# Layer A's probabilities turned by VectorE and transfers instead of TensorE, with k in runs of 32 tokens

## What is computed

```python
qkv = (x @ a_w_qkv[layer]).reshape(B, S, 3, A_HEADS, A_HEAD_DIM)
q = partial_rotary(qkv[:, :, 0], positions).transpose(0, 2, 1, 3)
k = partial_rotary(qkv[:, :, 1], positions).transpose(0, 2, 1, 3)
v = qkv[:, :, 2].transpose(0, 2, 1, 3)
o = moba_attention(q, k, v).transpose(0, 2, 1, 3).reshape(B, S, D)
x = layer_norm(DEEPNORM_ALPHA * x + o @ a_w_o[layer], ln_g[layer, 0], ln_b[layer, 0])
...
s_own = jnp.einsum("bhqd,bhkd->bhqk", qc, k_own) * scale   # masked causally
p = softmax(s_own)
o = jnp.einsum("bhqk,bhkd->bhqd", p, v)
```

## Time and profile before

| | |
|---|---|
| median of 3 runs (lowest, highest) | 606.54 us (605.67, 606.56) |
| profiled execution: device time | 606.49 us |
| its span in the trace | 604.7 us |
| mean granted TensorE clock | 0.996 of full speed |
| first mixer, from the first scores to the last transposes of probabilities | 48.7 to 102.6 us |
| HBM read | 108.23 MB, 181 GB/s over the span |

### The profile page before, as it was taken

The page is one execution under the profiler, slowest core; times in us unless marked ns, Lnnn a source line. Parts: engine busy times, 40 slices in busy tenths (PEclk is TensorE's granted clock), DMA queues, the critical chain, the costliest instruction groups (busy, mean ns, idle before and its releaser), DMA issues.

```text
span 604.7 us, 8638 instructions
## 1 busy us (share of the span) xinstructions
PE 594.5 (98%) x3252; PEld 503.9 (83%) x3252; DVE 456.6 (76%) x817; ACT 328.3 (54%) x532; POOL 56.1 (9%) x83
## 2 busy tenths in 40 slices
PE   8999999999999999999999999999999999999995
PEld 6877777898888888889878888889888888888894
DVE  4877864877777887777688797778777777777756
ACT  5666776355544445455436587945555455554430
POOL 6200000400000000000520003132000000000002
PEclk9999999999999999999999999999999999999998
DMA  8898643253666676555537965442845556755501
GB/s 309 283 301 255 190 139 140 89 207 122 209 209 209 209 234 239 185 182 189 199 102 240 295 159 206 140 139 72 277 158 190 184 183 221 248 189 187 181 1 69
DMA packets 86709, 114.03 MB, mean 189 GB/s; under 512 B 19292, under 2 KB 64652, under 8 KB 86668
## 3 DMA queue, kind: packets, MB, share of 16 engines
q1 hardware_dynamic: 85228, 109.28, 54.7%
q0 software_dynamic: 1152, 4.19, 2.1%
q10 hardware_dynamic: 288, 0.00, 0.0%
HBM read 108.23 MB, written 1.05 MB: 181 GB/s over the span
## 4 chain that ended last, share of the span: by engine, by line
PE 91%; DVE 3%; DMA 2%; POOL 2%; issue 1%; ACT 1%; DVEq 0%; ACTq 0%
PE wide L1215 16%; PE wide L1217 16%; PE wide L1216 16%; PE score L1400 11%; PE score L1403 6%; PE turn L1400 5%; PE outb L1400 5%; PE outb L1403 3%; PE turn L1403 3%; DMA raw<-in_a_w_qkv 1%; PE turn L1302 1%; DVE w_lo L917 1%; PE outb L1320 1%; PE score L1217 1%; PE score L1216 1%
## 5 line engine op out<-in xcount | busy, mean ns | idle before, releaser
L917 DVE TENSOR_TENSOR w_lo<-raw,w_hi 128x2048 fp32r<-128x2048 f32 (+1 forms) x118 | 209.0, 1788 | 70.7 <-ACT w_hi L726 70.7
L726 ACT ACTIVATE w_hi<-raw 128x2048 fp32r<-128x2048 f32 (+1 forms) x126 | 182.2, 1483 | 32.3 <-PE wide L1217 23.2
L1215 PE MATMUL wide<-w_hi,xT 128*128 128x512 f32 (+1 forms) x256 | 96.2, 376 | 1.3 <-DVE w_lo L983 0.7
L1215 PE MATMUL wide<-w_hi,oT_hi 128*128 128x512 f32 x240 | 95.5, 398 | 0.2 <-DVE oT_lo L1162 0.2
L1216 PE MATMUL wide<-w_lo,oT_hi 128*128 128x512 f32 x240 | 93.7, 390 | 0.0
L1217 PE MATMUL wide<-w_hi,oT_lo 128*128 128x512 f32 x240 | 93.6, 390 | 0.0
L1217 PE MATMUL wide<-w_hi,xT 128*128 128x512 f32 (+1 forms) x256 | 93.1, 364 | 0.0
L1216 PE MATMUL wide<-w_lo,xT 128*128 128x512 f32 (+1 forms) x256 | 93.0, 363 | 0.0
L1400 PE MATMUL score<-xT,w_hi 128*128 128x512 f32 x288 | 71.8, 391 | 0.0
L848 ACT ACTIVATE qT<-kT,conv_cols 128x256 f32<-128x256 f32 x36 | 21.7, 602 | 87.7 <-DVE kT L1128 87.7
L1400 PEld LDWEIGHTS score<-xT,w_hi 128*128 128x128 f32 x288 | 52.8, 188 | 10.1
(11 more groups left out here) (176 smaller groups left out, 805.3 us busy)
## 6 DMA issues: line engine op xcount, KB each, us to landing
raw<-in_ffn_w_in SPq DMA_DIRECT2D x44, 1024.0 KB, 5.2
raw<-in_ffn_w_out SPq DMA_DIRECT2D x22, 1024.0 KB, 5.0
raw<-in_a_w_qkv SPq DMA_DIRECT2D x9, 1024.0 KB, 6.6
raw<-in_w_kv_shared SPq DMA_DIRECT2D x8, 1024.0 KB, 5.7
raw<-in_a_w_o SPq DMA_DIRECT2D x4, 1024.0 KB, 4.8
raw<-in_b_w_q SPq DMA_DIRECT2D x4, 1024.0 KB, 5.1
raw<-in_b_w_o SPq DMA_DIRECT2D x4, 1024.0 KB, 5.1
raw<-in_a_w_qkv SPq DMA_DIRECT2D x4, 512.0 KB, 7.8
```

The source lines that it names most:

```text
L726: ins = nc.scalar.activation(w_hi[c % RING][:, part], raw[c % RAW_RING][:, part], ACT.Copy)
L917: ins = nc.vector.tensor_tensor(w_lo[c % RING][:, part], raw[c % RAW_RING][:, part], w_hi[c % RING][:, part].bitcast(F32), ALU.subtract)
L1215: nc.tensor.matmul(dst, a_hi, b_hi, start=start, stop=False, skip_group_check=True)
```

## The change

The three transposes per map on TensorE and the copy on ScalarE leave the first mixer. In their place VectorE turns a map's 384 columns in 32x32 tiles with one instruction (`prob_turn`, L1103 of the changed kernel), writing so that the 32-query blocks of four maps (a **set**; `BATCH` is 4) lie together. Each 32x32 tile takes every fourth column of `probs`. Once four maps are turned, SyncE moves the set with four SBUF-to-SBUF transfers of 32 partitions each (`prob_move`, L559), 1.5 KB a partition. There are two buffers at each end (`STAGES` is 2): the sets leave from `norm_rows` (later the gain and shift of the norm) and `turned` (shared with q and k), and arrive in `probsT` and in a new buffer, `spare`, in which the small buffers of the second mixer have been put. Since a tile takes every fourth column, the key tokens come out in another order, and k (not q) is laid out in `kT` in runs of 32 tokens where tokens were interleaved. The moving operand of the scores is then four runs of 32 for each token tile.

In the planner, `prob_turn` and `prob_move` take the place of `probT` and `probT_out`, loads have become steps of their own on SyncE, and the tables of numbers are new, for both layers: the second mixer is computed by the same instructions as before, but they stand in another order.

```diff
+BATCH, STAGES = 4, 2
...
-    "move": ("SP", 5.0),
+    "move": ("SP", 3.1),
+    "load": ("SP", 0.4),
+    "prob_turn": ("DVE", 0.6),
+    "prob_move": ("SP", 3.1),
...
+        add(("load", c + RAW_RING), ("split_lo", c, 1))
...
-        add(("exp", m), ("mask", m), ("probT", m - 4 if A else m // 2 - 2))
+        add(("exp", m), ("mask", m), ("prob_turn", m - 4) if A else ("probT", m // 2 - 2))
...
+        if A:
+            add(("prob_turn", m), ("norm", m), ("prob_move", m // BATCH - STAGES))
+            if m // BATCH % 2 and BATCH == 4:
+                after[("prob_turn", m)].append(("move", max(n for n, (mat, _) in enumerate(COLUMNS) if mat < 2)))
+            if m % BATCH == BATCH - 1:
+                n = m // BATCH
+                add(("prob_move", n), ("prob_turn", m), *[("pv", PAIR_GROUP[h // 2]) for h in range(BATCH * n - 8, BATCH * n - 8 + BATCH) if h >= 0])
+        elif m % 2:
...
-            add(("pv", n), *[("probT_out", h) for h in PV_GROUPS[n]], ("drain", column(2, g), 1), ("out_lo", n - 1))
+            add(("pv", n), ("prob_move", PV_GROUPS[n][-1] // BATCH), ("drain", column(2, g), 1), ("out_lo", n - 1))
...
+        spare = sb("spare", [P, BATCH * 3 * P])
...
+        probsT_A = [probsT[:, :, :].rearrange("p s k -> p (s k)"), spare[:, :]]
...
+        prob_stage = [norm_rows[:, 0:BATCH * 3 * P], turned[:, :, :, :].rearrange("p n b q -> p (n b q)")[:, 0:BATCH * 3 * P]]
+        prob_stage = [stage.rearrange("p (b s k q) -> p b s k q", b=4, s=BATCH, k=3) for stage in prob_stage]
...
-                    sp.dma_start(headT[mat][:, 4 * g:4 * g + 4, 64 * a:64 * a + 64],
+                    into = headT[1][:, 4 * g + a, :] if mat else headT[0][:, 4 * g:4 * g + 4, 64 * a:64 * a + 64]
+                    sp.dma_start(into,
                                  turned[32 * a:32 * a + 32, rank(cg) % 2, :, :]).then_inc(moved[mat, g], 16)
...
+            def prob_move(n):
+
+                sp.wait_ge(prob_turned, BATCH * (n + 1))
+                if n >= 2:
+                    sp.wait_ge(pv_done, BATCH * (n - 1))
+                for a in range(4):
+                    part = slice(a * BATCH * 3 * 32, (a + 1) * BATCH * 3 * 32)
+                    sp.dma_start(probsT_A[n % 2][:, part],
+                                 prob_stage[n % 2][32 * a:32 * a + 32].rearrange("p b s k q -> p b (s k q)")
+                                 ).then_inc(prob_moved[n % 2], 16)
+
...
-                    pool.wait_ge(proj_drained, 12)
+                    pool.wait_ge(prob_moved[0], 64 * (MAPS // BATCH // 2))
...
-                            act.wait_ge(turn_filled, fill_of[(0, "probT", m - 4)] + 1)
+                            act.wait_ge(prob_turned, m - 3)
...
-                        parts = turned[:, n % 2, :, :].rearrange("p b (t q s) -> p b t q s", t=4, s=ST)
+                        parts = turned[:, n % 2, :, :]
+                        parts = (parts.rearrange("p b (t s q) -> p b t q s", t=4, s=ST) if mat else
+                                 parts.rearrange("p b (t q s) -> p b t q s", t=4, s=ST))
...
+                    elif kind == "prob_turn":
+                        n = m // BATCH
+                        dve.wait_ge(norm_done, m + 1)
+                        if n >= 2:
+                            dve.wait_ge(prob_moved[n % 2], 64 * (n // 2))
+                        elif n == 1:
+                            for column_moved in moved.values():
+                                dve.wait_ge(column_moved, 64)
+                        nc.vector.transpose(prob_stage[n % 2][:, :, m % BATCH, :, :].rearrange("p b k q -> p k b q"),
+                                            probs[:, m % 4, :].rearrange("p (k i b) -> p k b i", k=3, b=4)
+                                            ).then_inc(prob_turned, 1)
...
+                            k_parts = headT[1][r, 4 * g:4 * g + 4, :].rearrange("p a (t s q) -> p t s a q", t=4, s=ST)
+                            return headT[0][r, tile, :].rearrange("p (n s) -> p s n", s=ST), k_parts[:, tile % 4]
...
-                                nc.tensor.matmul(scores[:, P:3 * P], qT[:, 1, :], kT[:, :, :], start=True,
+                                nc.tensor.matmul(scores[:, P:3 * P], qT[:, 1, :], kT, start=True,
...
-                        pe.wait_ge(turn_drained, fill_of[(layer, "probT", newest)] + 1)
+                        if layer == 0:
+                            n = newest // BATCH
+                            pe.wait_ge(prob_moved[n % 2], 64 * (n // 2 + 1))
+                        else:
+                            pe.wait_ge(turn_drained, fill_of[(1, "probT", m)] + 1)
...
+                            turned_probs = probsT_A[newest // BATCH % 2].rearrange("p (a s k q) -> p s k a q", a=4, s=BATCH, k=3)
...
-                                                     probsT[:, (head + h) % 4, 0:SEQ], start=n == 0, stop=False,
+                                                     turned_probs[:, (head + h) % 4, 0:2], start=n == 0, stop=False,
```

81 lines of the change are left out of this document (43 added, 38 removed).

## The result

| | before | changed |
|---|---|---|
| median of 17 runs each (lowest, highest) | 605.75 us (605.54, 610.35) | 608.2 us (606.98, 611.1) |
| ratio changed / before, 95% interval | | 1.0036 [1.0025, 1.0047] |
| profiled execution: device time, span | 606.49, 604.7 us | 607.55, 605.7 us |
| mean granted TensorE clock | 0.996 | 0.995 |

The change makes the kernel 0.36% slower, some 2.2 us, where I forecast 602.3 us, 0.7% faster than the 606.5 us that my sum started from. (The median of before over 17 runs is 0.75 us lower than that start, which explains none of the miss.) Of the changed kernel's 17 runs eight lie at 607.0 to 607.6, eight at 608.2 to 609.2 and one above; the profiled one is in the lower group. The runs of before lie at 605.5 to 606.6 but for one, and the profiled one is 0.7 us above their median. So the two traces differ by 1.0 us where the medians differ by 2.5.

What follows compares the result with a forecast made beforehand. TensorE, busy 594.5 of 604.7 us, was taken as the bound: 606.5 - 5.3 for triples + 0.8 for pv 3's wait + 0.3 for small waits = 602.3 us. The range was 600.9 to 604.9 us, about 2 in 10 outside.

Steps and rivals of the forecast that it cites:

- Removed triples: TensorE in the first mixer: 16 triples of transposes gone, 13 at 0.34 and 3 at 0.28 us, saving 5.3 us.
- The read of every fourth element: VectorE's new transposes of 384 elements a partition: 0.48 us each despite reading every fourth element.
- the ends: Bounds for one new VectorE transpose: short end 0.46 to 0.48 us, long end, a read at half rate, 0.88 us.
- (b): Rival: VectorE is the bound, transposes at 0.88 us delay scores 3, out_lo and pv 3; about 607.6 us; chance 0.13.
- The landing of the fourth set: SyncE's four transfers: landed 5.5 us after the set's last transpose, 3.4 to 6.2 at the extremes; here at 96.9 us.
- GpSimd's loads: First norm load now waits for set 2; costed at nothing, as nothing needs it before the output products end.
- The wait at pv 3: TensorE at pv 3, due at 96.3 us, waits for the fourth set: about 0.8 us including 0.2 for the restart.
- the flaw: Planner at pv 3: the fourth set's move does not exist as a step yet, so the need for it is dropped.
- some 3 us: Upper bound of TensorE's wait at pv 3, for a transpose at 0.6 us; the lower bound was 0.
- allowed 0.3: Allowance of 0.3 us in the sum for small waits at masks and chunk splits, with margins all 1 to 2 us.
- (c): Rival: transposes at 0.6 to 0.75 us, or transfers slowed by loads, landing on pv 3; 603.4 to 605.3 us; chance 0.14.
- The k layout: Scores' moving operand on TensorE, from every second element to runs of 32: gains nothing.

Runs made afterwards that it cites:

- e7: e3 with 16 triples of 128x128 transposes put back on TensorE, writing to the unused bank, nobody waiting for them: 606.2 us, 1.0005 of before.
- e3: Changed kernel with one more need in the planner's list, pv 3 after the move of the fourth set: 602.8 us, 0.9933 of before.
- e1: Changed kernel with the probabilities' turn reading 32 neighbouring columns per tile, so attention uses permuted keys: 605.8 us, 0.9990 of before.
- e8: e3 plus probabilities read in runs of 32, scores reading every eighth element of k, norm's loads behind the fourth set: 606.4 us, 1.0010 of before.
- e4: Changed kernel with k laid out as in the kernel before, every second element, in both layers: 609.3 us, 1.0049 of before.
- e2: Changed kernel with 18 matmuls on finished data put ahead of pv 3's wait: 606.1 us, 0.9994 of before.
- e9: Changed kernel with GpSimd's loads of the norm's gain and shift waiting for the fourth set, not the third: 609.5 us, 1.0059 of before.
- e13: Changed kernel with SyncE issuing nothing behind the fourth set until it has landed: 609.1 us, 1.0056 of before.
- e14: e1 with SyncE issuing nothing behind the fourth set until it has landed: 604.1 us, 0.9972 of before.
- e16: The changed kernel measured once more, unaltered: 608.1 us, 1.0041 of before.
- e6: Changed kernel with the fourth set moved in two halves, maps 12 and 13 first, then 14 and 15: 607.7 us, 1.0025 of before.
- e10: e6 with the norm's loads behind the second half of the fourth set: 602.8 us, 0.9954 of before.
- e12: e3 with the norm's loads waiting for the fourth set: 603.8 us, 0.9970 of before.
- e5: e1 with the norm's loads waiting for the fourth set, not the third: 603.8 us, 0.9966 of before.
- e11: e8 with k written at its turn on VectorE so that the scores read runs of eight: 600.4 us, 0.9910 of before.

## Why the prediction was wrong, point by point

**Removed triples: right.** 5.3 us by 0.34 each, 0.356 measured (e7). Scores 3 came 32.91 us behind scores 0, with 32.9 in my sum. e3, with a well placed pv 3, has 602.8 us, near my forecast; but its transposes take 0.77 us and not 0.48, so that is no proof of my sum.

**The read of every fourth element: wrong, 0.77 us instead of 0.48.** This is the term that failed first. The arithmetic on the elements was good (0.47 us for a dense read in e1), the choice between the ends was not. The group's mean was 0.85 to 0.87 us, near the 0.9 that I had named as the sign of (b). I let a reduction that reads PSUM speak for a transpose that reads SBUF, because it was the only jumping row on VectorE. The rule that I quoted against it, of the Trainium skill's "SBUF - State Buffer", section "Door 1: The DMA port swizzle", stood for the right side here: every fourth float32 of SBUF costs 0.3 us of 0.77, and TensorE's read of every eighth in e8 takes 637 ns where one of runs takes 380, while every second costs next to nothing on TensorE (e4). The rule fits these rows in direction. It doesn't settle the mechanism, for no run here varied the distance in steps. Nor was there the disagreement that I saw in the same section: its sentence on PSUM's 8-byte lines speaks of matmuls, and the reduction of the earlier trace rows runs on VectorE. So nothing stood against the rule but a row of another memory.

**The landing of the fourth set: mis-sized, 6.2 us and up instead of 5.5.** I took the moves of k as the price and let the threefold run length and the larger set cancel. Issues cost what I said (3.05 us for four). But the way from the first issue to the last landing varies by 1.6 us between traces: 6.2 to 7.8 us over the changed kernel, e1, e2, e4, e9, e13, e14 and e16. I had no term for it, and I had costed GpSimd's loads, now beside this set, at nothing. For the half set they cost 4 to 5 us (e6 against e10); for the whole set no run shows that they matter. **What makes the whole set's way vary stays open**: neither the loads beside it (e9) nor those behind it (e14) explain it alone, and no run took both away.

**The wait at pv 3: right in place and cause, 4.4 us instead of 0.8.** My sum turned the set at 91.4; it was issued at 95.0, 3.6 us late, and landed 0.8 us later still. That is 4.4 us late, and pv 3 itself came 0.6 us later than I had it. That the planner's missing need is what the slow read hurt through is shown by e3: two lines take the kernel from 608 to 602.8 us without making any instruction faster. I had named the flaw but priced it at 0.8 us, with "some 3 us" as its bound.

**The clock: missing.** No term, no rival. A wait of 0.8 us would not have needed one (e3, e10 and e12 wait up to 1.0 us there at full clock), but my bound of 3 us did: 2.1 us were enough in e5. With the wait that was measured my sum gives 602.3 + 3.6 + 0.6 = 606.5 (the 0.6 is the wait for oT_lo, 0.9 us where I had allowed 0.3), just the time that it started from; the lower clock, 1.57 us in the changed kernel's trace, carries it to 608.1. So the read and the landing used up the gain, and the clock made it a loss. e2 brings 2 us back.

**Rivals.** (b), the slower case, had the mechanism: a slow read whose cost lands on out_lo and pv 3, at 607.6 us. Its deciding point, 0.85 us a transpose, was wrong, since it counted on 2 us of idle time on VectorE, on a landing of 5.5 us and on a constant clock; 0.77 was enough. (c), 0.6 to 0.75 us, would by the same omissions probably have come out later than its 603.4 to 605.3; no run shows it. The k layout was right: nothing for TensorE (e4).

**What would have helped.** My sum had a steep side: each 0.1 us on the transpose moves pv 3 by up to 1.6 us, and the clock makes it worse. With such a slope, an unseen access pattern deserved more than 0.27 for both rivals on that side.

## What to carry to other kernels

When work moves off the bound engine onto one that has little idle time, look for the one consumer whose slack ends first, and ask whether the scheduler knows what it waits for: here one missing edge turned a gain of 0.7% into a loss of 0.4%. An access pattern that no row shows should be priced from the same memory as the row it is borrowed from; a gather can be moved to a place where nobody waits for it, as to k's own turn here. And an idle stretch of 2 us and more on TensorE cost more than its length here, so a bound of a wait needs the clock's term beside it.

## What the runs showed of the hardware

- A VectorE transpose of 128x384 float32 in SBUF takes 0.47 us in sequence from neighbouring elements and 0.77 us from every fourth. Writing every eighth element makes a 128x512 turn of k take up to 1.16 us instead of 0.69 (e11).
- A 64x256 float32 matmul takes a median of 380 ns with a moving operand of runs of 32 (changed kernel) or of eight (e11), 386 to 388 with every second element (before, e4), and 637 with every eighth (e8).
- Behind 2.1 to 5.9 us without work the granted clock was at its lower level for 3 to 6 us, with no plain relation between the two: 3.0 us behind 5.5 us of waiting in e16, 5.9 us behind the same in e4. In e5 and e13 the first matmuls behind the wait still ran at full speed and the slow ones followed. Behind waits of up to 1.0 us it stayed up (e3, e10, e12). The Trainium skill's "TensorE: Matmul & The Clock Gate", section "Part 1: The HAM clock gate", says that the number of slow matmuls at the start of one and the same kernel differs from run to run. In the middle of the changed kernel it is so too: 3.5 us of the lower clock in its first trace, 3.0 in e16's. 18 matmuls whose results nobody needs, issued in the wait, keep it up (e2).
- Four SBUF-to-SBUF transfers of 192 KB, issued within 3.0 to 3.4 us, have all landed 6.2 to 7.8 us after the first issue; beside 1 MB of loads from GpSimd's queue, eight of 96 KB took up to 8.0 us each, and up to 4.8 without (e6, e10).
